# Six modulation blocks at the head of a two-layer transformer kernel, moved from VectorE to TensorE

## The reference, cut to what matters

```python
c_act = jax.nn.silu(c)                                   # c is 1 x 1024
mod = (c_act @ ada_w[i] + ada_b[i])[:, None, :]          # ada_w[i] is 1024 x 6144
sh1, sc1, g1, sh2, sc2, g2 = jnp.split(mod, 6, axis=-1)
h = rmsnorm(x, mix_norm_pre[i]) * (1.0 + sc1) + sh1
y = windowed_gqa_sink(h, att_w_qkv[j], att_w_o[j], att_sink[j], rel_bias)
```

## Time and profile before

| what | value |
| --- | --- |
| time, median of 3 runs | 2032.34 us |
| time of the profiled execution | 2028.85 us |
| its span | 2026.7 us |
| TensorE matmuls | 1725.1 us busy, 85% of the span |
| VectorE | 1468.2 us busy, 72% |
| ScalarE | 920.2 us busy, 45% |
| GpSimd | 624.9 us busy, 31% |
| DMA | 723.25 MB, 357 GB/s in the mean |
| first q, k, v matmul starts | 36.96 us after the span's start |
| first scores of attention | 61.53 us |

### The profile page before, as it was taken

How to read it: one execution, slowest core, us unless ns; L and a number is a source line. 1 busy time by engine, 2 the same in 40 slices (tenths; PEclk the granted TensorE clock), 3 DMA queues, 4 the chain that set the end, 5 groups by cost and what they waited for, 6 DMA issues and landing times.

```text
span 2026.7 us, 22047 instructions
## 1 busy us (share of the span) xinstructions
PE 1725.1 (85%) x6989; PEld 1017.8 (50%) x6989; DVE 1468.2 (72%) x3271; ACT 920.2 (45%) x2398; POOL 624.9 (31%) x575
## 2 busy tenths in 40 slices
PE   4979998999896999987778778998999877778776
PEld 3759996988775544432233223454555322223222
DVE  7778888898876678666776776356877776777675
ACT  4664444445654445444444444334444444444443
POOL 1540000000004444343434443114445434443431
PEclk9989999999998999999999999999999999999999
DMA  9666677777749999999999999759999999999996
GB/s 384 264 228 229 249 281 271 270 251 249 268 162 359 420 421 421 421 420 418 422 421 421 422 421 421 265 203 409 419 417 420 421 421 422 421 421 421 421 422 255
DMA packets 119404, 723.25 MB, mean 357 GB/s; under 512 B 12012, under 2 KB 13828, under 8 KB 43000
## 3 DMA queue, kind: packets, MB, share of 16 engines
q0 software_dynamic: 75152, 541.35, 64.5%
q1 hardware_dynamic: 44136, 180.50, 24.2%
HBM read 720.72 MB, written 1.08 MB: 356 GB/s over the span
## 4 chain that ended last, share of the span: by engine, by line
DMA 39%; PE 30%; DVE 18%; ACT 5%; issue 4%; POOL 4%; SPq 0%; DVEq 0%; ACTq 0%; POOLq 0%
DMA X<-in_k_uv,EI 23%; PE PS L2321 12%; DMA Z<-in_k_uv,EI 10%; PE PS L2007 4%; DVE junk L1994 4%; PE PS L2009 3%; PE PS L2008 3%; PE PS L2297 3%; DMA W<-in_k_uv,EI 3%; DVE HALF L1614 2%; POOL X L1114 2%; DVE WL L1626 2%; DMA HALF<-in_k_ada 2%; DMA W<-in_k_ada 2%; PE PS L2338 1%
## 5 line engine op out<-in xcount | busy, mean ns | idle before, releaser
L2321 PE MATMUL PS<-X,dg 128*128 128x512 f32 x1380 | 663.6, 614 | 129.7 <-ACT dg L1123 127.0
L1994 DVE CUSTOM_DVE_ANT_0 junk<-H,X 128x1024 f32<-128x1024 f32 x345 | 422.0, 1223 | 236.9 <-DMA X<-in_k_uv,EI 222.1
L1114 POOL DMA_INDIRECT X<-in_k_uv,EI x345 | 369.4, 1071 | 509.2 <-PE PS L2321 361.4
L2321 PEld LDWEIGHTS PS<-X,dg 128*128 128x128 f32 x1380 | 248.4, 193 | 502.1 <-ACT dg L1123 281.6
L1123 ACT ACTIVATE CF<-DOT 128x1 f32<-128x1 f32 x512 | 103.6, 202 | 646.9 <-DVE DOT L1994 641.8
L2321 PE MATMUL PS<-Z,dg 128*128 128x512 f32 x480 | 233.7, 614 | 53.4 <-ACT dg L1123 53.0
L1123 ACT ACTIVATE dg<-CP,CG 128x128 f32<-128x128 f32 x512 | 205.6, 401 | 20.2 <-PE PS L2321 3.6
L1994 DVE CUSTOM_DVE_ANT_0 junk<-H,Z 128x1024 f32<-128x1024 f32 x120 | 146.9, 1224 | 88.4 <-DMA Z<-in_k_uv,EI 85.0
L2007 PE MATMUL PS<-XH,WH 128*128 128x256 f32 x592 | 172.3, 291 | 13.3 <-DVE WL L1626 12.0
L2321 PEld LDWEIGHTS PS<-Z,dg 128*128 128x128 f32 x480 | 84.1, 190 | 184.7 <-ACT dg L1123 117.3
L2008 PE MATMUL PS<-XL,WH 128*128 128x256 f32 x592 | 168.7, 285 | 0.0
(11 more groups left out here) (320 smaller groups left out, 2587.5 us busy)
## 6 DMA issues: line engine op xcount, KB each, us to landing
HALF<-in_k_ada SPq DMA_DIRECT2D x66, 512.0 KB, 5.4
W<-in_k_ada SPq DMA_DIRECT2D x24, 1024.0 KB, 7.1
Y<-in_k_ada SPq DMA_DIRECT2D x15, 1024.0 KB, 7.1
W<-in_k_win SPq DMA_DIRECT2D x15, 1024.0 KB, 7.5
W<-in_k_ffi SPq DMA_DIRECT2D x13, 1024.0 KB, 6.4
Y<-in_k_ffi SPq DMA_DIRECT2D x9, 1024.0 KB, 6.3
W<-in_ffn_w_out SPq DMA_DIRECT2D x8, 1024.0 KB, 5.0
W<-in_peer_wq SPq DMA_DIRECT2D x8, 1024.0 KB, 12.3
```

Source lines behind the costliest of these rows:

```text
L1114: e.indirect_dma_start(out=WS[k][:, :], out_offset=None, in_=I[f"k_uv{ly}"][:, :], in_offset=bass.IndirectOffsetOnAxis(ap=EI[t][:, j:j + 1 ...
L1994: e.tensor_tensor_reduce(junk, H[:, t, :], d[:, 0:D], 1.0, 0.0, ALU.mult, ALU.add, DOT[:, j:j + 1]).then_inc(v_dot, 1)
L2321: p = e.matmul(PS[:, 2 * t + q, :], dgb[n % 4][:, :], d[:, D + q * 512:D + (q + 1) * 512], start=(j == 0), stop=(j == 127))
```

## The change

In the list, the head is written anew. New steps are `cc`, `lds1` (the loads of `small1`, moved ahead), `adp` m (block m on TensorE) and `ldc2`.

- c is loaded as one row of 4 KB (`crow`). TensorE turns it into a column by 8 products with a 1 x 1 operand, and spreads it to all partitions by 2 products with a row of ones. ScalarE takes silu of both from PSUM: `ccol` and `CB[0]`.
- Blocks 2 to 7 are stored transposed in DRAM, and `adp` multiplies each with `ccol`: 2 chunks of 8 f32 matmuls, 128 x 128 weights and one moving column each. VectorE's `mod` adds the bias straight from PSUM. Blocks 0 and 1 stay on VectorE, as do all blocks from 8 on.
- Only the identity is loaded at the head. The other 784 columns of `CP` and the second block's c vectors are requested by SP (`ldc2`), in the list at unit 12 of attention.
- BE is loaded in two halves, the second issued when the first has landed. `ldw` 0 is also loaded in two halves.
- The odd chunks of `xt` for the first x go to VectorE, the even ones stay on ScalarE. The first quarters of product 0 take all high parts first, and then the low part of the weights.

The diff, cut to its core:

```diff
-    three, first = (0, 1, 2), (0, 1, 2, 4, 5, 6, 7, 3)
+    three, first = (0, 1, 2), (0, 1, 2, 4, 5, 6, 7, 6)
     P("init")
+    P("cc")
+    P("lda", 0)
+    P("lda", 1)
+    P("lds1")
+    for m in range(2, 5):
+        P("lda", m)
     P("rms", 0)
     P("normed", 0)
     for c in range(8):
-        if c < 7:
-            P("xp", 0, c, first[c])
-    after = {0: "small1", 2: "bias", 3: "small2"}
-    for m in range(6):
-        ada(m, 0)
-        ada(m, 1)
-        if m in after:
-            P(after[m])
-    P("xp", 0, 7, 3)
+        P("xp", 0, c, first[c])
+    for m in range(2):
+        for j in range(2):
+            P("ada", m, j)
+    P("small1")
+    P("adp", 2)
+    P("bias")
+    P("lda", 5)
+    P("adp", 3)
+    P("lda", 6)
+    P("adp", 4)
+    P("small2")
+    P("lda", 7)
+    P("adp", 5)
+    P("ldw", 0)
     P("mod", 0)
     P("g", 0)
-    ada(6, 0)
-    P("lda", 7)
-    P("ldw", 0)
+    for c in range(6):
+        P("xt", 0, c, first[c])
+        if c > 1:
+            P("xl", 0, c - 2)
+    P("adp", 6)
     P("ldw", 1)
     P("be")
-    for c in range(3):
-        P("xt", 0, c, first[c])
-    ada(6, 1)
-    for c in range(3):
-        P("xl", 0, c)
-    P("ada", 7, 0)
-    P("ada", 7, 1)
+    P("xl", 0, 4)
+    P("xl", 0, 5)
+    P("adp", 7)
+    P("split", 0, 0)
+    P("split", 0, 1)
     P("mod", 1)
     P("g", 1)
-    P("xt", 0, 3, first[3])
-    P("split", 0, 0)
     P("low", 0, 0)
-    P("xl", 0, 3)
-    for c in (4, 5):
-        P("xt", 0, c, first[c])
-        P("xl", 0, c)
-    P("split", 0, 1)
-    P("low", 0, 1)
     for c in (6, 7):
         P("xt", 0, c, first[c])
-        P("xl", 0, c)
+    P("xl", 0, 6)
+    P("xl", 0, 7)
+    P("low", 0, 1)
     split(1)
...
+        if n == 12:
+            P("ldc2")
...
-        return i == 0 or c % 2 == 1
+        return c % 2 == (i > 0)
...
+        crow = CB[1][0:1, :]
...
+            if kind == "lda" and 2 <= a[0] < 8:
+                return p_ada, a[0] + 1
...
                 if kind == "init":
-                    e.dma_start(CB[0], spread(I["c"][0:1, :])).then_inc(d_c, 16)
+                    e.dma_start(crow, I["c"][0:1, :]).then_inc(d_c, 16)
                     e.dma_start(XS[:, :, :], I["x"].rearrange("b (t p) d -> p (b t) d", p=128)).then_inc(d_x, 16)
-                    e.dma_start(CP[:, :], I["k_cp"]).then_inc(d_cp, 16)
-                elif kind == "small1":
+                    e.dma_start(ident, I["k_cp"][:, 0:128]).then_inc(d_cp, 16)
+                elif kind == "ldc2":
+                    w.wait_ge(d_cp, 16)
+                    e.dma_start(CP[:, 128:912], I["k_cp"][:, 128:912]).then_inc(d_cp, 16)
+                    w.wait_ge(d_td, 16)
+                    e.dma_start(CB[1], spread(I["c_2"][0:1, :])).then_inc(d_c2, 16)
+                    e.dma_start(CB[2], spread(I["c_ctx_2"].rearrange("(a b) -> a b", a=1))).then_inc(d_c2, 16)
+                elif kind == "lds1":
                     w.wait_ge(g_init, 1)
...
-                    if kind == "ldw":
+                    if (kind, *a) == ("ldw", 0):
+                        w.wait_ge(d_x, 16)
+                        e.dma_start(d[:, 0:1024], part_src(0)[:, 0:1024]).then_inc(d_x, 16)
+                        e.dma_start(d[:, 1024:2048], part_src(0)[:, 1024:2048]).then_inc(d_slot[k], 16)
+                    elif kind == "ldw":
...
                     w.wait_ge(*slot("ldw", 1)[1:])
-                    e.dma_start(BE[:, :, :], bass.AP(tab_d, 0, [[1, 128], [512, 16], [1, 384]])).then_inc(d_be, 16)
-                    e.dma_start(CB[1], spread(I["c_2"][0:1, :])).then_inc(d_c2, 16)
-                    e.dma_start(CB[2], spread(I["c_ctx_2"].rearrange("(a b) -> a b", a=1))).then_inc(d_c2, 16)
+                    for i in range(2):
+                        if i:
+                            w.wait_ge(d_be, 16)
+                        e.dma_start(BE[:, 8 * i:8 * i + 8, :],
+                                    bass.AP(tab_d, 4096 * i, [[1, 128], [512, 8], [1, 384]])).then_inc(d_be, 16)
...
                 if kind == "init":
-                    w.wait_ge(d_c, 16)
-                    act(CB[0], CB[0], ACT.Silu).then_inc(a_cs, 1)
+                    w.wait_ge(g_init, 2)
+                    act(mg[:, 0:1], ones[:, 0:1], ACT.Silu)
+                elif kind == "cc":
+                    w.wait_ge(p_ada, 1)
+                    act(ccol[:, :], PS[:, 3, 0:8], ACT.Silu).then_inc(a_cs, 1)
+                    w.wait_ge(p_ada, 2)
+                    act(CB[0], PS[:, 6:8, :].rearrange("p a b -> p (a b)"), ACT.Silu).then_inc(a_cs, 1)
...
+                    if n + i == 0:
+                        w.wait_ge(d_x, 32)
+                    else:
+                        w.wait_ge(arrived, count)
...
-                    w.wait_ge(a_cs, 1 if m < 24 else 3)
+                    w.wait_ge(a_cs, 2 if m < 24 else 4)
...
-                    w.wait_ge(v_ada, nth("ada", MOD_LAST[s], 1))
                     w.wait_ge(v_small, 1 if s < 5 else 3)
-                    e.tensor_tensor(dst, dst, bias, ALU.add).then_inc(v_mod, 1)
+                    if s < 2:
+                        lo, hi = ((2, 6), (6, 8))[s]
+                        both = [x[:, o:o + 16].rearrange("p (a c) -> p a c", a=2)
+                                for x, o in ((MC[0], 0), (C1, c_ab), (PS[:, 7 if s == 0 else 3, :], 256))]
+                        w.wait_ge(p_ada, hi)
+                        d, z, x = (y[:, :, lo:hi] for y in both)
+                        q = e.tensor_tensor(d, x, z, ALU.add)
+                        if s == 0:
+                            w.wait_ge(v_ada, nth("ada", 1, 1))
+                            d, z = (y[:, :, 0:2] for y in both[:2])
+                            q = e.tensor_tensor(d, d, z, ALU.add)
+                        q.then_inc(v_mod, 1)
+                    else:
+                        w.wait_ge(v_ada, nth("ada", MOD_LAST[s], 1))
+                        e.tensor_tensor(dst, dst, bias, ALU.add).then_inc(v_mod, 1)
...
-                    w.wait_ge(d_be, 16)
+                    w.wait_ge(d_be, 16 + 16 * s2)
...
+                if (n, q % 2) == (0, 0):
+                    o = PS[:, b + 2 * m, m * 256:(m + 1) * 256]
+                    w.wait_ge(a_hi, 1)
+                    for k in range(4):
+                        z = slice(k * 256 + m * 128, k * 256 + m * 128 + 128)
+                        turned(i, k)
+                        e.matmul(o, h[:, z], xh[:, k, :], start=(k == 0), stop=False)
+                        e.matmul(o, h[:, z], xl[:, k, :], start=False, stop=False)
+                    w.wait_ge(v_lo, 1)
+                    for k in range(4):
+                        z = slice(k * 256 + m * 128, k * 256 + m * 128 + 128)
+                        p = e.matmul(o, l[:, z], xh[:, k, :], start=False, stop=False)
+                    return p
...
+                if kind == "cc":
+                    w.wait_ge(g_init, 2)
+                    w.wait_ge(d_c, 16)
+                    for k in range(8):
+                        p = e.matmul(PS[:, 3, k:k + 1], crow[:, k * 128:(k + 1) * 128], ones[0:1, 0:1], start=True, stop=True)
+                    p.then_inc(p_ada, 1)
+                    for i in range(2):
+                        p = e.matmul(PS[:, 6 + i, :], ones[0:1, :], crow[:, i * 512:(i + 1) * 512], start=True, stop=True)
+                    p.then_inc(p_ada, 1)
+                    free[3], free[6], free[7] = [(a_cs, 1)], [(a_cs, 2)], [(a_cs, 2)]
+                elif kind == "adp":
+                    m = a[0]
+                    b = 7 if m < 6 else 3
+                    d, arrived, count = slot("lda", m)
+                    w.wait_ge(arrived, count)
+                    w.wait_ge(a_cs, 1)
+                    if m == 6:
+                        take(3)
+                        free[3] = [(v_mod, nth("mod", 1))]
+                        free[7].append((v_mod, nth("mod", 0)))
+                    for j in range(2):
+                        o = 256 + COLUMNS[m][j]
+                        for k in range(8):
+                            p = e.matmul(PS[:, b, o:o + 1], by_k(d, 8)[:, k, j * 128:(j + 1) * 128], ccol[:, k:k + 1],
+                                         start=(k == 0), stop=(k == 7))
+                    p.then_inc(p_ada, 1)
+                elif kind == "small1":
...
+    for m in range(2, 8):
+        arrays["k_ada"][m] = ada[0, list(COLUMNS[m])].reshape(2, 128, 8, 128).transpose(3, 2, 0, 1).reshape(128, 2048)
```

More of the change, by code:

```diff
@@ L787, in build @@
         ones, one8 = sb("ones", [128, 128]), sb("one8", [128, 8])
+        ccol = sb("ccol", [128, 8])
         zero8, gn8 = sb("zero8", [128, 8]), sb("gn8", [128, 8])
@@ L840, in heads, with turning @@
             return ap.rearrange("p (a b) -> p a b", a=8)
+        def turning(i, c):
+            return 256 if (i, c) == (0, 7) else 0
         units = [(s2, i, t) for s2 in range(2) for i in range(4) for t in range(2)]
@@ L856, in build @@
              "tt", "pq", "rt", "dg", "pi", "band", "grp", "po", "w"))
```

(24 more changed lines are left out.)

## The result

| | before | after |
| --- | --- | --- |
| median, runs beside each other (4 each) | 2033.26 us | 2055.26 us |
| span of the profiled execution | 2026.7 us | 2054.1 us |
| first product of q, k, v | 36.96 us | 62.50 us |
| first scores of attention | 61.53 us | 88.17 us |
| second unit of attention on VectorE (the mark) | 67.41 us | 91.29 us |

The ratio of the times is 1.0108, with an interval from 1.0096 to 1.012: the changed kernel is 22 us slower. The forecast was 2032.6 us with a range up to 2035.0, so the result lies far outside it.

What follows compares the result with a forecast made beforehand. The head was taken as bound by VectorE until 37, TensorE until 61.5, and DMA throughout. Delays of 2.7 + 0.1 + 0.5 less 3.0 us got back gave +0.3 on 2032.34: 2032.6 us, range 2026.2 to 2035.0.

Steps and rivals of the forecast that it cites:

- What bounds the kernel: Only the first 75 us matter, setting when attention starts; candidates VectorE until 37, TensorE until 61.5, DMA over all of it.
- Step 1: VectorE in the head loses 12 of its 16 modulation instructions, 13.8 us of work.
- Step 2: TensorE gains 96 one-column f32 products at 0.21 us each: 3.4 us a block, 20.4 us for six.
- Step 3: Queue start, c through TensorE: squares of x at 9.1 instead of 7.96, transposes at 12.9 instead of 11.86.
- Step 4: TensorE's queue from 12.9: product 0 at 39.7 instead of 36.96, 2.7 us later, plus 0.1 us lost.
- Step 5: Product 0 gets 2.4 GHz after 4 us instead of 3.1, costing 0.45 us; first scores at 64.8.
- Step 6: 1.95 MB less DMA, so BE and block 11 are not late; second unit at 67.7 against 67.41, +0.3 us.
- Step 7: Costed at nothing: moved `ldc2` (3.5 us without cover), BE in halves, SP's waits, the `xt` split.
- The fast rival: Block products raise the clock or cost half, 1.8 us a block; DMA binds, second unit -5.3 us, 2027.0 us; chance 0.27.
- the rival's last sentence: On what raises TensorE's clock in the head: by the skill's page, transposes do not count, so they decide little.
- The slow rival: Block products' loads don't overlap, 0.29 us each: 7.7 us more ahead of product 0, 2040 us; chance 0.10.

Runs made afterwards that it cites:

- e8_bf16_halves: Changed kernel with blocks 2 to 7 multiplied using only the upper 16 bits of each weight and a bf16 column of silu(c): 2026.77 us, ratio 0.9969.
- e2_half_k: Changed kernel with only the first four of eight products per column, 48 products instead of 96: 2034.43 us, ratio 1.0017.
- e4_wide: Changed kernel with 128 equal moving columns instead of one in each block product, everything computed: 2036.80 us, ratio 1.0020.
- e6_later_consts: Kernel before with only the later constants and second block's c requested in attention, and BE in two halves: 2028.61 us, ratio 0.9979.
- e1_all_dve: Changed kernel with blocks 2 to 7 back on VectorE, the rest of the change kept: 2032.95 us, ratio 1.0005.
- e3: Changed kernel with 64 instead of 128 weight columns in each block product, one small product added at the head: 2034.62 us, ratio 1.0017.
- e7: Changed kernel with only blocks 2 and 6 on TensorE, the other four back on VectorE: 2034.32 us, ratio 1.0015.
- e10: e6_later_consts with the first low half of the weights ahead of the second instruction of block 7 on VectorE: 2028.24 us, ratio 0.9978.
- e9: e5 with the first low half of the weights ahead of block 7 in VectorE's queue: 2031.79 us, ratio 0.9994.
- e5: Changed kernel with all eight blocks on VectorE and c spread over the partitions by DMA as before: 2031.20 us, ratio 0.9991.

## Why the prediction was wrong

- *What bounds the kernel.* Right: only the head matters, and the distance at the mark stays through attention.
- *Step 1.* Right. The 12 instructions left VectorE, and VectorE idled.
- *Step 2 is the one that failed.* It priced an f32 product at one load, 0.21 us. The price of an instruction was right, 0.213; the number of instructions per product was not. A product is two loads and two passes, 0.43 us, so a block costs 6.83 us instead of 3.4, and the six 41.0 instead of 20.4. The trace of before had shown it: one call of the bias product stands in the earlier trace rows as L2093 x2, and its loads in the earlier trace rows are x2 as well. I read the 1.86 us there as the price of two products. And the f32 stream of the earlier trace rows, from which the 0.21 came, had the same count in it: I took the x13 and x16 of L2297 as products, but they are instructions. The source makes 352 such calls and the trace of before has 704 of their matmuls, so 13 of them are six and a half products. The other source, the slope of the load, is the price of one load and says nothing of how many a product needs. By the Trainium skill ("TensorE: Matmul & The Clock Gate", "LDWEIGHTS (loading the stationary operand)") a load of 128 columns would be 0.107 us, and no type is named there; the runs show 0.213 for f32 at 1.2 GHz and at most 0.027 for bf16. The section behind it on weight-path modes says that a faster load is taken with 128 weights of any type but f32; e8_bf16_halves agrees with that.
- *Step 3* has the same fault. The column took 3.54 us instead of 1.7 and the spread row 3.76 instead of 1.86, so the squares of x started at 12.03 instead of 9.1 and the transposes at 15.16 instead of 12.9.
- *Step 4.* The queue was right, its numbers not: product 0 at 62.50, predicted 39.7. The difference is 6 x (6.83 - 3.41) = 20.5 from step 2 and 2.3 from step 3, 22.8 in all, which is what was measured. e2_half_k, with a block at 3.41 us, had product 0 at 41.94: 39.7 and step 3's 2.3 us give 42.0. A block costs TensorE more than VectorE's 2.3 us at either level of the clock (6.8, and 3.6 in e4_wide).
- *Step 5.* The clock rose 5.6 us after product 0 began, predicted 4. The first scores came 25.67 us after product 0, before 24.57: 1.1 us lost, 0.5 predicted.
- *Step 6.* Right in kind: no DMA wait ahead of the second unit. e6_later_consts shows it alone, 2.35 us at the mark. In the changed kernel it is buried. The sum has a slip of 0.2 us: without the waits 67.41 becomes 64.6, so 2.8 us come back and not the 3.0 of the sum.
- *Step 7.* Not contradicted: `ldc2` went out at 96.98 us, and nothing waited for it.
- *The fast rival* needed products that raise the clock or cost half. TensorE was busy for 46.9 of the 47.3 us from 15.2 to 62.5, 41 of them with one-column products of 0.213 us each, and that did not raise the clock. The Trainium skill's rule on sustained matmul activity (the same page, Part 1) doesn't hold for them here. Nor do transposes decide as little as the rival's last sentence had it: in e1_all_dve the clock rose at 18.8 us, and behind an idle stretch of 5.61 us TensorE had done nothing but transposes (from 15.25). But the rival's arithmetic is borne out where a block is cheap: it said second unit between 61.1 and 62.7 and 2027.0 us, and e8_bf16_halves gives 61.68 and 2026.77, with blocks of 0.6 us where the rival had 1.8; the agreement to a few tenths is luck.
- *The slow rival* had the right sign and the wrong cause. Its point of decision, 0.25 us a product, was passed by far at 0.43. By its own scale, 96 products with 0.22 us more than the forecast's are 21 us.

Why a product with f32 operands is two instructions, and why each takes 0.213 us where a bf16 one takes 0.027, is not something these runs explain. They show the size of it.

## What to carry to other kernels

Count instructions, not calls: the xN of a row in the trace, over the number of calls in the source, is the first factor of any new matmul's price, and for products with f32 operands it was 2, for transposes and for products on rounded parts 1. A matrix-vector product on TensorE pays for loading all of its weights and gets nothing back from a short moving side: with f32 weights a megabyte cost 6.8 us at 1.2 GHz, more than VectorE's 2.3 us and DMA's 2.5, with only the upper 16 bits of each weight 0.6. And test the parts of a mixed change alone: here the moved loads gained 4 us while the moved products lost over 20.

## What the runs showed of the hardware that was not expected

- The load of 128 bf16 columns with its one-column product takes 0.027 us from start to start, an f32 product 0.427: a factor of 16 at the same clock (e8 against after). At 2.4 GHz the bf16 one takes 0.025, so it hardly goes with the clock, while the f32 instruction with 128 columns goes from 0.213 to 0.112 (e4).
- A full TensorE did not by itself get 2.4 GHz here: in after it was busy for 46.9 of 47.3 us, mostly with one-column products, and stayed at 1.2 GHz. With 128 moving columns the same products kept the 2.4 GHz that they found when they began (e4).
- In e1, e4 and e8 the clock rose at 18.2 to 18.8 us, with the 16 f32 transposes going on or just done; in after, e2, e3 and e7 it did not, with the same transposes started within 0.6 us of the same time. After and e8 even give TensorE the same work up to there and start it at the same time (15.16), so the kernel alone does not decide it. In e1 and e8 it fell again at 22 us, as TensorE had little to do.
- From the start of product 0 to the rise to 2.4 GHz it took 3.1 us (before), 4.4 (e6), 5.3 (e2, e3), 5.6 (after) and 5.8 (e10), with no pause of TensorE in between. In e9, with 2.02 us without work at 40.5, the rise came 3.7 us later than in e5. One execution of each, against such a spread, does not show that the pause is the cause.
